# A recurrence on pairs of tokens, and a softmax unit that is scaled in its own round, in the mixer of a two-block network

## The reference, cut to what matters

```python
# attention, for each head, kind of key and block of 128 query rows
e = exp(s - max(s)); p = gate * e / sum(e); o += p @ v
# S5
a_bar  = exp(lam * dt)                         # complex, 32 x 64
bu     = (u @ b_re + 1j * u @ b_im) * (a_bar - 1) / lam
state  = scan(state[t] = a_bar * state[t-1] + bu[t])      # over 512 tokens
y      = re(state) @ c_re - im(state) @ c_im + d * u
y      = gelu(y); out = y * sigmoid(y @ w_glu + b_glu)
```

## Time and profile before

| | before |
|---|---|
| median of 3 runs | 2065.24 us (2062.25 to 2070.86) |
| profiled execution | 2072.4 us, span 2070.5 us |
| busy in the span: PE, DVE, ACT, POOL | 1975.8 (95%), 1247.4 (60%), 846.2 (41%), 387.3 (19%) us |
| chain that ended last | PE 77%, DVE 16%, ACT 4%, issue 2%, POOL 1%, DMA 1% |

### The profile page before, as it was taken

How to read it: one execution, slowest core, us unless ns; L and a number is a source line. 1 busy time by engine, 2 the same in 40 slices (tenths; PEclk the granted TensorE clock), 3 DMA queues, 4 the chain that set the end, 5 groups by cost and what they waited for, 6 DMA issues and landing times.

```text
span 2070.5 us, 21878 instructions
## 1 busy us (share of the span) xinstructions
PE 1975.8 (95%) x8614; PEld 1516.5 (73%) x8614; DVE 1247.4 (60%) x1646; ACT 846.2 (41%) x1269; POOL 387.3 (19%) x343
## 2 busy tenths in 40 slices
PE   7999999989977899999999999999999899999997
PEld 5888888766532478888888777776788778766786
DVE  6764344597796445655664776925773468536742
ACT  5331333201445633322333446645552357455531
POOL 2000000156244010100001202512400013214102
PEclk9999999998778899999999989999999999999998
DMA  4232232221000124554552222222122222220221
GB/s 185 85 126 82 95 107 97 85 64 71 26 0 1 66 79 164 196 202 148 198 200 75 82 91 80 82 82 82 52 91 92 97 83 82 91 83 31 92 92 61
DMA packets 53317, 196.69 MB, mean 95 GB/s; under 512 B 5984, under 2 KB 6496, under 8 KB 52704
## 3 DMA queue, kind: packets, MB, share of 16 engines
q1 hardware_dynamic: 43200, 160.55, 22.3%
q0 software_dynamic: 7504, 28.58, 4.1%
q10 hardware_dynamic: 2512, 6.18, 0.9%
HBM read 192.14 MB, written 2.10 MB: 94 GB/s over the span
## 4 chain that ended last, share of the span: by engine, by line
PE 77%; DVE 16%; ACT 4%; issue 2%; POOL 1%; DMA 1%; SPq 0%; POOLq 0%; DVEq 0%; ACTq 0%
PE PS L571 76%; DVE AR L1590 3%; DVE WLO L1587 3%; DVE AR L1823 2%; DVE AR L2072 1%; ACT WHI L1116 1%; PE PS L790 1%; DVE TMP L2146 1%; DVE AR L1913 1%; DVE AR L2039 0%; DVE HNL L1590 0%; DVE ACC L1590 0%; DMA RAW<-in_w13a 0%; DVE H L1975 0%; POOL ACC L2322 0%
## 5 line engine op out<-in xcount | busy, mean ns | idle before, releaser
L1587 DVE TENSOR_TENSOR WLO<-RAW,WHI 128x1024 fp32r<-128x1024 f32 (+1 forms) x272 | 378.3, 1394 | 509.2 <-ACT WHI L1116 509.2
L571 PE MATMUL PS<-HNH,WHI 128*128 128x512 f32 x1632 | 657.9, 403 | 16.0 <-ACT HNH L1147 14.1
L571 PE MATMUL PS<-HNH,WLO 128*128 128x512 f32 x1632 | 640.6, 393 | 3.8 <-DVE WLO L1587 3.8
L1116 ACT ACTIVATE WHI<-RAW 128x1024 fp32r<-128x1024 f32 (+1 forms) x272 | 297.6, 1095 | 648.0 <-PE PS L571 577.1
L571 PE MATMUL PS<-HNL,WHI 128*128 128x512 f32 x1632 | 436.7, 390 | 0.4
L571 PEld LDWEIGHTS PS<-HNH,WHI 128*128 128x128 f32 x1632 | 308.6, 189 | 96.9 <-issue 22.3
L571 PEld LDWEIGHTS PS<-HNH,WLO 128*128 128x128 f32 x1632 | 308.8, 189 | 78.7 <-issue 9.3
L571 PEld LDWEIGHTS PS<-HNL,WHI 128*128 128x128 f32 x1632 | 307.3, 188 | 66.4 <-DVE HNL L1590 2.6
L2202 POOL TENSOR_TENSOR ACC<-ACC,SQ 128x512 f32<-128x512 f32 x46 | 62.9, 1367 | 786.4 <-ACT SQ L1131 785.4
L571 PE MATMUL PS<-AR 128*128 128x512 f32 (+12 forms) x652 | 181.9, 515 | 6.5 <-DVE SQ L1807 5.8
L571 PEld LDWEIGHTS PS<-AR 128*128 128x128 f32 (+5 forms) x652 | 86.3, 203 | 76.8 <-issue 53.0
(11 more groups left out here) (314 smaller groups left out, 2475.6 us busy)
## 6 DMA issues: line engine op xcount, KB each, us to landing
RAW<-in_w_in SPq DMA_DIRECT2D x80, 512.0 KB, 3.5
AR<-in_w_ada POOLq DMA_DIRECT2D x48, 512.0 KB, 3.8
RAW<-in_w13a SPq DMA_DIRECT2D x44, 512.0 KB, 3.2
RAW<-in_w13b SPq DMA_DIRECT2D x44, 512.0 KB, 4.2
RAW<-in_w_out SPq DMA_DIRECT2D x40, 512.0 KB, 3.5
RAW<-in_w2a SPq DMA_DIRECT2D x16, 704.0 KB, 4.1
RAW<-in_w2b SPq DMA_DIRECT2D x16, 704.0 KB, 5.5
RAW<-in_w_inA SPq DMA_DIRECT2D x12, 512.0 KB, 3.3
```

The source lines that it names most:

```text
L571: return pe.matmul(o, l, r, start=start, stop=stop, skip_group_check=True)
L1116: act.activation(hi_of(name, i), raw_of(name, i), ACT.Copy).then_inc(*HI.up(name, i))
L1587: dve.tensor_tensor(lo_of(name, i), raw_of(name, i), f32(hi_of(name, i)), S_).then_inc(*LO.up(name, i))
```

## The change

Recurrence. The tokens are taken in pairs. With a = a_bar, the state at odd tokens follows state[t+1] = a^2 * state[t-1] + (a*b) u[t] + b u[t+1], so the scan runs over 256 pairs: 2 pieces of 128 in place of 4, with decay and angle squared. `U` is kept with its 256 even tokens first, then the 256 odd. The output at an odd token is read from the state as before (`CpR`, `CpI`); the output at an even token is read from the state one pair earlier with the matrix c*a (`CaR`, `CaI`) plus a direct term of that token's input (`THRU`).

Effects on the steps: "scan" 2 pieces; "drive" PE 8 multiplications of 256 columns for both tiles at j = 0, DVE 2 products of 512 columns for each tile, POOL two sums of 256; "back" DVE one product of 256, POOL one of 256 and one of 512; "read" PE 17 multiplications of 255 or 256 columns. A block has 8 steps, S5 64. The new constants cost, in feed-forward a, more pieces of `s5_params` (DVE 12 products of 512 columns and 6 copies out of PSUM) and, after hidden tile 6, `s5_weights` on PE: 8 transposes and 32 multiplications of 128 by 32 by 32.

Order. "scale" of unit n now stands in round n, after "scores" and one S5 step; the second S5 step comes at the round's end. "flip" stays two rounds behind. 34 of the 64 steps come before round 0 again, so the last is in round 14; "gelu" stays in round 23.

Placement. `OL` moves over the place of `CB`, so the load of `c` for the second block waits for the last `w_out` tile. The parameter load `s5_bc` has 3072 in place of 2048 columns, in two transfers.

```diff
 def s5_order():
-            for c in range(4):
+            for c in range(2):
...
 def mix_order():
             if n > 32:
-                yield ("scale", *work[n - 2])
                 yield ("out_s5",)
             yield ("flip", *work[n - 2])
...
         if n < 32:
-            if n:
-                yield ("scale", *work[n - 1])
             yield ("scores", *work[n])
+            yield from some(1)
+            yield ("scale", *work[n])
...
-        yield from some(2)
+        yield from some(1)
...
+            def s5_weights():
+                for z, src in enumerate((ATr, ATi)):
+                    ps, b = take(pe, "s5_a", z)
+                    pe.wait_ge(*V.at("s5_at"))
+                    for y4 in range(4):
+                        t = pe.transpose(ps[:, P * y4:P * y4 + P], src[:, 4 * y4:4 * y4 + 4, :].rearrange("p a b -> p (a b)"), IDENT)
...
+                for t16 in range(16):
...
+                    mm(o, BTr[:, t16, :], CpR[:, t16, :], True, False)
+                    t = mm(o, BTi[:, t16, :], CpI[:, t16, :], False, True)
...
                 elif step == "drive":      # PE
-                    mm(psR[:, :], SBr[r, y4, :], U[r, y4, :], True, True)
-                    mm(psI[:, :], SBi[r, y4, :], U[r, y4, :], True, True)
+                    if j == 0:
+                        for half, (even, odd) in enumerate(((SAr, SBr), (SAi, SBi))):
+                            for e, w in enumerate((even, odd)):
+                                for x, (ps, _) in enumerate(bs):
+                                    ts[x] = mm(ps[:, HT * half:HT * half + HT], w[r, y4, :], U[r, y4, HT * e:HT * e + HT], e == 0, e == 1)
...
                 elif step == "read":       # PE
+                    mm(ps[r, 0:HT], THRU[r, y4, r], U[r, y4, 0:HT], True, False)
                     for z in range(4):
-                        for j in range(2):
+                        for now in (True, False):
+                            for j in range(2):
...
+                                if now:
+                                    t = mm(o[:, HT:T], w[:, t16, :], x, False, z == 3)
+                                else:
+                                    t = mm(o[:, 1:HT], w[:, t16, :], x[:, 0:HT - 1], False, z == 3)
...
                 elif step == "drive":      # DVE
-                    dve.tensor_tensor(f4(vr), f4(psR[:, :]), c4, M_).then_inc(*V.up("drive_a", t16))
-                    dve.wait_ge(*P_.at("drive_im", t16))
-                    dve.tensor_tensor(f4(t1), f4(psI[:, :]), s4, M_).then_inc(*V.up("drive_b", t16))
-                    dve.tensor_tensor(f4(vi), f4(psI[:, :]), c4, M_).then_inc(*V.up("drive_im", t16))
-                    dve.tensor_tensor(f4(t2), f4(psR[:, :]), s4, M_).then_inc(*V.up("drive", t16))
+                    dve.tensor_tensor(f4(V_[b % 2][:, j, :]), f4(ps[:, :]), c4, M_)
+                    dve.tensor_tensor(f4(S5T[j]), f4(ps[:, :]), s4, M_)
...
+            pool.wait_ge(*P_.at("w_out", KD - 1))
             pool.dma_start(CB, D["c"].partition_broadcast(P))
```

198 lines of the change are left out of this document (126 added, 72 removed).

## The result

| | before | after |
|---|---|---|
| median | 2063.7 us | 2031.3 us |
| lowest to highest | 2061.6 to 2070.9 | 2026.5 to 2033.5 |
| ratio, 95% interval | 1 | 0.983, 0.980 to 0.987 |
| profiled execution, its span | 2072.4, 2070.5 us | 2029.7, 2027.9 us |
| mean granted clock | 0.96 | 0.98 |

The kernel got 32 us faster by the medians; forecast was a time of 2030 us. The forecast's sum, 41 us less, started from the profiled execution of before, which at 2072.4 us lies above the highest of before's four, 2070.9; from that one to the profiled execution after it is 43. Executions of the kernel before differ by their clock: in 13 of them the granted clock goes from 0.968 (2061.7 us) to 0.963 (2071.0 us).

What follows compares the result with a forecast made beforehand. Bound: PE outside the mixer; inside, waits made by DVE's queue, S5 above all, with PE's low clock around them. 5 - 13 - 28 - 5 = -41 gives 2031 from 2072.4 or 2024 from 2065.2; forecast 2030 us, range 2015 to 2045.

Steps and rivals of the forecast that it cites:

- four terms: Feed-forward a +5 us, stretch before round 0 -13, rounds 0 to 22 -28, the rest of the mixer -5.
- Part 4: Tiles qk and v before round 0: waits for DVE's full queue go, 93 us in place of 106, -13 (-5 to -17).
- Part 5: Rounds 0 to 22: scaling waits go, PE becomes fullest engine, 115 us in place of 143, -28; bounds 95 and 133.
- Part 6: Mixer from 666 to 741 us: some of PE's 10.0 us behind the scaling goes, -5 us (-12 to +3).
- Part 1: DVE's S5 work in the mixer: scans, drives, backs and carries fall from 142 to 70 us, 72 less.
- Part 2: PE's S5 work: a read 3.9 us, a drive pair 1.8 to 2; 89 us before round 0, 80 in rounds 0 to 22.
- PE pays for each instruction: Rival, chance 0.08: weight loads of PE's half-length multiplications aren't hidden, +15 us, 2085 us, slower than before.
- Part 3: New constants in feed-forward a: PE's transposes and small multiplications +5 us (3 to 9), DVE's twelve products 0.
- 96 + 9 + 10: Rounds 0 to 22: 96 us PE work at clock 0.83, 9 remaining idle, 10 from DVE's waits in reads; 115 us.
- The low clock: Rival, chance 0.18: PE's clock stays low in the mixer's rounds, -15 us in all, 2057 us.
- DVE's load is not what holds the mixer: Rival, chance 0.10: squeeze, transfers and ACT's order hold the rounds, waits only change their names; 2066 us.
- All of it: Rival, chance 0.14: PE at full clock nearly throughout, -69 us, 2001 us.

Runs made afterwards that it cites:

- e1: The changed kernel with the round's old order, so only the recurrence on pairs is left: 2019.9 us, 0.977 of the time before.
- e8: The kernel before with DVE's and POOL's S5 work about halved and the shorter list of scan steps, PE's S5 work unchanged: 2019.1 us, 0.978.
- e9: Pairs with the old order, DVE's twelve products for new constants spread over two steps in place of one: 2014.2 us, 0.976 of the time before.
- e7: The kernel before with DVE's S5 work about halved and two scan steps a block in place of four, POOL's work whole: 2038.5 us, 0.986.
- e11: The kernel before with only POOL's S5 instructions cut to 256 of 512 columns from the third block on: 2053.2 us, 0.995.
- e5: Pairs with the old order, but DVE makes the factor in the unit's own round while ACT scales one round later: 2022.4 us, 0.979 of before.
- e4: The changed kernel, but from round 24 on the factor and scaling stand one round later, as before: 2030.1 us, 0.982 of the time before.
- e3: The kernel before with only DVE's S5 work about halved, half of the tokens not scanned: 2038.2 us, 0.986.
- e2: The kernel before with only the new order of a round, the recurrence still on single tokens: 2075.3 us, 1.004.

## Why the prediction was right, and where it wasn't

The time was right, in part by luck. The way it was to come about, less load on DVE and fewer waits and more clock for PE, held. Of its four terms three had the right sign. Against the profiled execution of before, Part 4 gave 5.8 us more than forecast and Part 5 1.9 more, Part 6 6.3 less: these errors cancel. From median to median the gain is 32 us and not 41; the forecast hits because of the two times that the sum gave, 2031 and 2024, it took nearly the higher one.

- **Part 1 (DVE 142 to 70 us)** held: 71 us. In the stages: 66.6 us before round 0 (69 forecast), 56.7 + 10.5 = 67.2 in rounds 0 to 22 (63). I expected the mean scan more likely to fall; it stayed at 612 ns, and rose to 662 in e1: shorter instructions of POOL meet a larger share of the scans (15 and 22 of 64, 26 of 128 before). So the new order spares DVE some 3 us of scans, and the kernel is slower with it all the same. The Trainium skill ("SBUF — State Buffer", "Who interferes with whom") has it that a DVE instruction with two inputs in SBUF and a POOL instruction that reads SBUF exclude each other. The traces agree that a scan beside POOL is slower (1179 ns against 438 after). That the halved scans would then save clearly over half, which I had worked out from it, doesn't show: 71.5 us went to 35.3, and to 38.5 in e1.
- **Part 2 (PE)** held for the instructions: 4.3 us a read (3.9 forecast), 2.00 a pair of drives. The rival in which PE pays for each instruction falls by the same rows, and e8, with PE's old form, is as fast. It didn't hold for the stages: PE's work at full clock is 86.6 us before round 0 (89 forecast) and 90.7 in rounds 0 to 23 (80 forecast).
- **Part 3 (+5)** was right by two errors. PE's own part is 1.9 us, not 5: the small multiplications were scaled by count from a row in which other costs stood. DVE's twelve products, priced at nothing because "the lag was worked off", cost 1.8 us of waiting and, in this execution, 1.7 of low clock. In the three executions of the same code in which the clock didn't fall the stage is 2.8 us longer than the mean of before (388.5), so that 4.9 came so near to 5 is luck as well. The pieces that stood there before lasted 7.5 us; this one lasts 9.5, and the lag didn't take it. e9 takes the wait back.
- **Part 4 (-13, bound -17)** was mis-sized: -18.8. I put PE's work at 89 us and left 4 us of idle or slow time; it was 86.6, and 1.0 is left. The reason, DVE's full queue, was half of it. DVE halved with the list of steps of the pairs (e7) brings only 2.6 us of this stage, as one block more stands there; POOL halved as well brings 12.7 more (e8), and by e11 POOL's load alone is worth 7. I had named POOL's busy time and not asked what its halving brings.
- **Part 5 (-28)** came out as -29.9, by a sum of a larger gain and a loss that I hadn't seen. Pairs alone give -37.1 (142.4 to 105.3), and the order gives 7.2 back. The sum 96 + 9 + 10 was right by errors that cancel: PE's work at full clock was 90.7 us and not 80 (I had taken all of the low clock as busy time before, and 88.5 were work there), the low clock took 7.6 and not 16, and idle time was 14.3 and not 19. The step that failed is what stands behind "What the move puts in its place": "DVE stands in the reciprocal until both exponentials are done; behind it are the round's second S5 step and the next maximum". I named what is queued behind the waiting reciprocal on DVE. The moved step has a second waiting instruction, ACT's scaling, and what is queued behind that on ACT, the copies, is what PE needs. Also, with pairs alone, all of PE's idle time in the rounds is 7.8 us: with a short DVE queue most of the wait for the late scaling went by itself (15.7 us to 7.1), and e5, with the factor a round earlier, gains nothing.
- **Part 6 (-5)** was wrong: +1.3. PE's 10.0 us behind the scaling became 2.7, and 4.9 behind DVE's copy (L2003), 3.2 behind ACT's copies and 2.9 behind the low halves came instead (the 3.2 behind DVE's reciprocal in the kernel before went); I had allowed 2 for the low halves. e4 shows that neither order shortens this stage.
- **The rivals.** The low clock didn't stay: 0.96 in rounds 0 to 15, 1.00 before. Transposes ran at the full clock in them, eight in 1.09 us (576.01 us in the kernel after), as before. What the Trainium skill says ("TensorE: Matmul & The Clock Gate", Part 4), that the full clock doesn't engage for transposes, isn't borne out for transposes amid other work; what transposes alone would do, no run here shows. "DVE's load is not what holds the mixer" falls by e3. "All of it", 2001, wasn't reached by any kernel; e9 came nearest. That "waits only change their names" was right for the order alone, where I had not looked for it: I judged the two parts of the change as one gain, and no case of the prediction had one of them negative.

What is open: how much of the order's cost in e2 is ACT's queue and how much DVE's wait; what a scaling with a ready factor ahead of the copies costs; and what sets the 113 us from round 23 on. Before, after and in e1 PE idles 14 us there and the low clock takes some 7; two edits of the order moved waits and gained nothing.

## What to carry over

A step that is moved has a waiting instruction on each engine that it touches; for each of them list what is queued behind it and who needs that, not only for the engine whose wait one wants to be rid of. A wait for an engine's result can come from that engine's own queue (here a gelu and its table load) and not from its input; then an earlier input buys nothing, and it is worth a look at the instructions ahead before the step is moved. When two edits come together, price each alone with its own sign, since a right sum can hide that leaving one out is better: here the kernel without the new order, and with the constants spread, takes 0.976 of the time where the change takes 0.983.

## What the runs showed of the hardware

- Very small multiplications cost little each: 32 of 32 columns took 0.86 us at the full clock, 27 ns each, where a row of 31 columns at the low clock had suggested 120.
- The same scan of 128 columns takes 438 to 456 ns in the mean when POOL is idle and 948 to 1284 when POOL runs beside it. The mean over all, 561 to 749 ns, goes by how many scans meet POOL and how long its instructions are; the order of the steps alone moved it from 662 to 612.
- Behind the same wait of 1.8 us in an otherwise unbroken stretch of PE the granted clock fell in three of six executions, to a mean of 0.57 to 0.60 over the next 4 us, and cost about as much again as the wait; in the other three it stayed at 1.00. One execution doesn't tell what such a wait costs.
- Of the 37 us that pairs alone take off rounds 0 to 23, 17.0 are idle time of PE and 22.5 what the low clock took; PE's work at the full clock is 2.4 us more.
